# Seven-product experts: another order of products and joins, later sums, a second slot for one weight quarter, an earlier gather

## The reference

```python
def expert_choice_moe(x, w_router, w_gate_up, w_down):
    B, S, _ = x.shape
    cap = CAPACITY_FACTOR * S // N_EXPERTS
    aff = jax.nn.softmax((x @ w_router).astype(jnp.float32), axis=-1)
    gates, idx = lax.top_k(jnp.swapaxes(aff, 1, 2), cap)
    bi = jnp.arange(B)[:, None, None]
    xs = x[bi, idx]
    g, u = jnp.split(jnp.einsum('becd,edf->becf', xs, w_gate_up), 2, axis=-1)
    out = jnp.einsum('becf,efd->becd', jax.nn.silu(g) * u, w_down) * gates[..., None].astype(x.dtype)
    return jnp.zeros_like(x).at[bi, idx].add(out)
```

## Time and profile before

| what | value |
|---|---|
| median of 3 runs | 4094.3 us (4091.58 to 4097.19) |
| profiled execution's own time | 4084.89 us |
| its span | 4083.2 us |
| TensorE busy | 3809.2 us (93%) |
| VectorE busy | 2042.4 us (50%) |
| ScalarE busy | 1127.0 us (28%) |
| GpSimd busy | 470.7 us (12%) |
| mean granted TensorE clock | 0.973 of full |

### The profile page before, as it was taken

How to read it: one execution, slowest core, us unless ns; L and a number is a source line. 1 busy time by engine, 2 the same in 40 slices (tenths; PEclk the granted TensorE clock), 3 DMA queues, 4 the chain that set the end, 5 groups by cost and what they waited for, 6 DMA issues and landing times. The chain is left out here.

```text
span 4083.2 us, 68182 instructions
## 1 busy us (share of the span) xinstructions
PE 3809.2 (93%) x28924; PEld 2006.4 (49%) x28924; DVE 2042.4 (50%) x3704; ACT 1127.0 (28%) x2409; POOL 470.7 (12%) x629
## 2 busy tenths in 40 slices
PE   8999999898989799999979999998999979999998
PEld 5555755757575644545544333333444444333333
DVE  2233334565656511146656566664366557566664
ACT  2343223434343301025531111113343421011113
POOL 3340002111111000000100111110000000111110
PEclk8998999999999999999989999999999989999999
DMA  4001101000100042020049899987211149899997
GB/s 107 27 26 39 33 27 47 9 22 9 27 4 22 4 143 78 11 62 1 1 181 325 298 322 314 315 316 275 74 37 31 52 170 320 282 324 319 326 325 255
DMA packets 271454, 567.51 MB, mean 139 GB/s; under 512 B 53504, under 2 KB 127392, under 8 KB 271152
## 3 DMA queue, kind: packets, MB, share of 16 engines
q1 hardware_dynamic: 255680, 506.01, 36.1%
q0 software_dynamic: 9504, 34.61, 3.2%
q10 hardware_dynamic: 5968, 22.55, 1.4%
HBM read 514.85 MB, written 48.23 MB: 138 GB/s over the span
## 5 line engine op out<-in xcount | busy, mean ns | idle before, releaser
L3618 PE MATMUL bank<-ring,m_hidden_T 128*128 128x512 f32 x1024 | 452.0, 597 | 0.0
L3618 PEld LDWEIGHTS bank<-ring,m_hidden_T 128*128 128x128 f32 x1024 | 192.4, 191 | 248.7 <-issue 248.7
L3618 PE MATMUL bank<-ring,m_picked_T 128*128 128x512 f32 x512 | 233.5, 614 | 4.1 <-ACT m_picked_T L3801 4.1
L1562 PE MATMUL bank<-hnT,first_block 128*128 128x336 f32 (+3 forms) x544 | 182.1, 487 | 8.0 <-PEq L101 7.3
L3631 PE MATMUL bank<-X,m_chosen 128*64 128x512 f32 x768 | 173.2, 604 | 6.3 <-POOL m_chosen L4210 6.3
L3631 PE MATMUL bank<-ring,m_chosen 128*64 128x512 f32 x768 | 174.2, 595 | 0.0
L4012 DVE TENSOR_TENSOR X<-ring 128x1024 f32<-128x1024 f32 x96 | 115.0, 1221 | 100.6 <-DMA ring<-in_moe_w_gate_up 99.7
L3618 PEld LDWEIGHTS bank<-ring,m_picked_T 128*128 128x128 f32 x512 | 99.3, 197 | 126.9 <-issue 121.5
L241 PE MATMUL bank<-xT,first_block 128*128 128x512 f32 x352 | 152.4, 593 | 2.8 <-ACT l_i L3269 1.7
L2825 PE MATMUL bank<-xT,a_weights 128*128 128x512 f32 x320 | 142.3, 595 | 0.8 <-ACT xT L2681 0.8
L1562 PEld LDWEIGHTS bank<-hnT,first_block 128*128 128x128 f32 x544 | 102.2, 193 | 66.0 <-issue 18.8
(11 more groups left out here) (554 smaller groups left out, 7093.7 us busy)
## 6 DMA issues: line engine op xcount, KB each, us to landing
ring<-in_moe_w_gate_up SPq DMA_DIRECT2D x512, 512.0 KB, 7.5
ring<-in_moe_w_down SPq DMA_DIRECT2D x256, 512.0 KB, 5.6
first_block<-in_w_in SPq DMA_DIRECT2D x23, 512.0 KB, 3.9
w_block<-in_w_in SPq DMA_DIRECT2D x19, 512.0 KB, 3.9
x_rows<-X ACTq DMA_DIRECT2D x2, 4096.0 KB, 17.3
ring<-y_rows SPq DMA_DIRECT2D x16, 512.0 KB, 8.7
out_w<-in_w_out ACTq DMA_DIRECT2D x11, 512.0 KB, 12.3
first_block<-in_lru_w_in SPq DMA_DIRECT2D x11, 512.0 KB, 3.9
```

The costliest lines, as they stand in the source:

```text
L1562: m = pe.matmul(banks[j][:, 0:n], wb[i % 3][:, d, :], hnT[:, d, col:col + n], start=d == 0, stop=d == KD - 1)
L3618: m = pe.matmul(banks[j][:, :], lhsT[:, (i % 8) * P:(i % 8 + 1) * P], ring[:, i, j, :], start=i % 8 == 0, stop=i % 8 == KD - 1)
```

## The change

- **Products**: s4b22, s2t2, s1t1, s3t3, 12b21; `turn_tokens(e + 1)`; 22t4; then the first half's transposes, half a product, the second half's. s1t1 goes into the bank of the first product, which first_kept has emptied. Columns 0 to 511 of `hid` are finished first, 512 to 1023 last.
- **Joins** in the order u2, c22's part (u4), 12, u3, 22, 11, 21; the gating of the first half before 22t4's join.
- **Sums**: all of t1, t2 and t3 of e+1 behind the last gating product.
- **Loads**: quarter 0 has a second set of slots (`m_second_ring`, 4 slabs), taken by even experts; it is loaded two experts ahead, slab by slab between down slabs. `landed` grows by 4 semaphores. All eight down slabs of e+1 are loaded as those of e are used.
- **ScalarE**: the first half's sigmoid before the token copies; both copies of the hidden halves after the second sigmoid.
- **GpSimd**: from expert 3 on, the gather of e+2 follows the sums of e+1, ahead of scatter e.

The diff, without its context lines and without the hunks that only pass the expert to `landed_at`, `quarter` and `weight`:

```diff
@@ -3411,7 +3411,7 @@
-        ring = st.sb("ring", [P, SLABS, 2, HALF_FF])
+        ring, second = st.sb("ring", [P, SLABS, 2, HALF_FF]), st.sb("m_second_ring", [P, 4, 2, HALF_FF])
...
@@ -3424,7 +3424,7 @@
-        landed = [st.sem(f"slab_landed{i}") for i in range(SLABS)]
+        landed = [st.sem(f"slab_landed{i}") for i in range(SLABS + 4)]
...
@@ -3449,8 +3449,8 @@
-        PRODUCTS = ("11", "s2t2", "s3t3", "s1t1", "22t4", "12b21", "s4b22")
-        JOINS = ("u2", "u3", "22", "u4", "21", "11", "12")
+        PRODUCTS = ("11", "s4b22", "s2t2", "s1t1", "s3t3", "12b21", "22t4")
+        JOINS = ("u2", "u4", "12", "u3", "22", "11", "21")
...
@@ -3488,9 +3488,15 @@
-        quarter = lambda q, j: ring[:, 4 * q + j, :, :].rearrange("p x c -> p (x c)")
+        place = lambda e, i: SLABS + i if e in SEVEN and e % 2 == 0 and i < 4 else i
+        slot = lambda e, i: (second[:, i, :, :] if place(e, i) >= SLABS else ring[:, i, :, :])
+        quarter = lambda e, q, j: slot(e, 4 * q + j).rearrange("p x c -> p (x c)")
...
+        def landed_at(e, i):
+            at = place(e, i)
+            return landed[at].sem, 16 * sum(place(x, i) == at for x in range(e + 1))
...
         def slab(e, i):
...
@@ -3508,7 +3514,7 @@
         def sync(sp):
             def load(e, i):
-                sp.dma_start(ring[:, i, :, :], slab(e, i)).then_inc(*landed[i].up(16))
+                sp.dma_start(slot(e, i), slab(e, i)).then_inc(*landed[place(e, i)].up(16))
...
@@ -3519,29 +3525,29 @@
+            for i in range(4):
+                load(SEVEN[0] + 1, i)
+            for i in range(20, SLABS):
+                sp.wait_ge(used.sem, used_at(SEVEN[0] - 1, i + 1))
+                load(SEVEN[0], i)
...
-                sp.wait_ge(w_summed.sem, w_summed_at(e, "t3_3"))
-                sp.wait_ge(made.sem, made_at(e, "11"))
-                for i in range(4):
+                sp.wait_ge(w_summed.sem, w_summed_at(e, "t2_3"))
+                sp.wait_ge(made.sem, made_at(e, "s4b22"))
+                for i in range(8, 12):
...
-                for i in range(20, SLABS):
-                    sp.wait_ge(used.sem, used_at(e - 1, i + 1))
-                    load(e, i)
...
+                sp.wait_ge(w_summed.sem, w_summed_at(e, "t4_3"))
...
-                sp.wait_ge(made.sem, made_at(e, "s4b22"))
-                for i in range(8, 12):
-                    load(e + 1, i)
-                for i in range(16, 20):
+                sp.wait_ge(w_summed.sem, w_summed_at(e, "t3_3"))
+                for i in range(16, SLABS):
+                    if e + 2 < NE and i < 20:
+                        load(e + 2, i - 16)
...
-            for i in range(20, SLABS):
-                sp.wait_ge(used.sem, used_at(NE - 2, i + 1))
-                load(NE - 1, i)
...
         def spread_bank(x, t):
...
@@ -3652,43 +3658,40 @@
-                        pe.wait_ge(joined.sem, joined_at(e - 1, "u3"))
-                m = product(first_bank(e), x_quarter(e, 0, 0), weight(0), (lo, hi))
+                        pe.wait_ge(joined.sem, joined_at(e - 1, "22"))
+                m = product(first_bank(e), x_quarter(e, 0, 0), weight(e, 0), (lo, hi))
...
-            def four_products(e):
+            def five_products(e):
...
+                pe.wait_ge(x_summed.sem, x_summed_at(e, "s4"))
+                landed_all(e, 2)
...
+                product(ps[3], summed(3), weight(e, 2)).then_inc(*made.up())
...
-                pe.wait_ge(x_summed.sem, x_summed_at(e, "s2"))
...
+                pe.wait_ge(kept.sem, e - SEVEN[0] + 1)
+                product(first_bank(e), summed(0), weight(e, 1)).then_inc(*made.up())
...
-                product(ps[3], summed(0), weight(1)).then_inc(*made.up())
+                pe.wait_ge(joined.sem, joined_at(e, "u4"))
+                landed_all(e, 3)
+                product(first_bank(e), x_quarter(e, 0, 1), weight(e, 3)).then_inc(*made.up())
...
+            def last_product(e):
...
-            def fifth_product(e):
...
-                pe.wait_ge(kept.sem, e - SEVEN[0] + 1)
-                landed_all(e, 3)
-                product(first_bank(e), x_quarter(e, 0, 1), weight(3)).then_inc(*made.up())
...
-            def last_product(e):
...
-                pe.wait_ge(joined.sem, joined_at(e, "u4"))
-                pe.wait_ge(x_summed.sem, x_summed_at(e, "s4"))
-                landed_all(e, 2)
-                product(ps[3], summed(3), weight(2)).then_inc(*made.up())
...
             def turn_half(e, i):
...
-                    m = pe.transpose(ps[4 + i][:, b * P:(b + 1) * P], hid[:, 512 * (1 - i) + b * P:512 * (1 - i) + (b + 1) * P],
+                    m = pe.transpose(ps[4 + i][:, b * P:(b + 1) * P], hid[:, 512 * i + b * P:512 * i + (b + 1) * P],
...
@@ -3725,11 +3728,10 @@
-                    four_products(e)
+                    five_products(e)
...
-                    fifth_product(e)
+                    last_product(e)
...
-                    last_product(e)
...
@@ -3805,22 +3807,18 @@
             def keep_first(e):
...
-                    ac.wait_ge(acted.sem, 4 * e - 1)
+                    ac.wait_ge(acted.sem, 4 * e - 3)
...
             def sigmoid_half(e, i):
-                if i == 0:
-                    ac.wait_ge(joined.sem, joined_at(e, "21"))
-                    ac.activation(hid[:, 512:1024], c21, ACT.Sigmoid).then_inc(*sig.up())
-                else:
-                    ac.wait_ge(joined.sem, joined_at(e, "11"))
-                    ac.activation(hid[:, 0:512], first_kept[:, :], ACT.Sigmoid).then_inc(*sig.up())
+                ac.wait_ge(joined.sem, joined_at(e, ("11", "21")[i]))
+                ac.activation(hid[:, 512 * i:512 * i + 512], (first_kept[:, :], c21)[i], ACT.Sigmoid).then_inc(*sig.up())
...
             def copy_half(e, i):
...
-                ac.activation(hs[:, :].rearrange("p (s b r t) -> p s b r t", s=2, b=4, r=2)[:, :, :, 1 - i, :],
+                ac.activation(hs[:, :].rearrange("p (s b r t) -> p s b r t", s=2, b=4, r=2)[:, :, :, i, :],
...
             def sigmoid(e, h):
@@ -3851,10 +3849,11 @@
+                    sigmoid_half(e, 0)
...
-                    for i in range(2):
-                        sigmoid_half(e, i)
-                        copy_half(e, i)
+                    sigmoid_half(e, 1)
+                    copy_half(e, 0)
+                    copy_half(e, 1)
...
@@ -4035,40 +4034,34 @@
-                ve.wait_ge(made.sem, made_at(e, "s3t3"))
+                ve.wait_ge(made.sem, made_at(e, "s1t1"))
...
-                ve.tensor_tensor(u3[:, :], third_bank(e)[:, :], u2[:, :], ALU.add).then_inc(*joined.up())
+                ve.tensor_tensor(c22[:, :], first_bank(e)[:, :], u2[:, :], ALU.add).then_inc(*joined.up())
+                ve.wait_ge(joined.sem, joined_at(e, "u4"))
+                ve.tensor_tensor(c12, ps[3][:, :], c22[:, :], ALU.add).then_inc(*joined.up())
...
-                ve.wait_ge(made.sem, made_at(e, "s1t1"))
-                ve.wait_ge(joined.sem, joined_at(e, "u3"))
-                ve.tensor_tensor(c22[:, :], ps[3][:, :], u3[:, :], ALU.add).then_inc(*joined.up())
-                ve.wait_ge(made.sem, made_at(e, "s1t1"))
-                ve.tensor_tensor(u2[:, :], ps[3][:, :], u2[:, :], ALU.add).then_inc(*joined.up())
+                ve.wait_ge(made.sem, made_at(e, "s3t3"))
+                ve.tensor_tensor(u3[:, :], third_bank(e)[:, :], u2[:, :], ALU.add).then_inc(*joined.up())
+                ve.tensor_tensor(c22[:, :], third_bank(e)[:, :], c22[:, :], ALU.add).then_inc(*joined.up())
+                ve.wait_ge(made.sem, made_at(e, "12b21"))
+                ve.tensor_tensor(first_kept[:, :], first_bank(e)[:, :], first_kept[:, :],
+                                 ALU.add).then_inc(*joined.up())
+                ve.wait_ge(joined.sem, joined_at(e, "11"))
+                ve.tensor_tensor(c12, c12, first_kept[:, :], ALU.mult).then_inc(*acted.up())
+                ve.wait_ge(sig.sem, 2 * e + 1)
+                ve.wait_ge(*acted.now())
+                ve.tensor_tensor(hid[:, 0:512], hid[:, 0:512], c12, ALU.mult).then_inc(*acted.up())
...
-                ve.wait_ge(sig.sem, 2 * e + 1)
+                ve.wait_ge(sig.sem, 2 * e + 2)
...
-                    sum_first(e + 1, 0)
-                    sum_first(e + 1, 1)
-                ve.wait_ge(made.sem, made_at(e, "12b21"))
-                ve.tensor_tensor(first_kept[:, :], first_bank(e)[:, :], first_kept[:, :],
-                                 ALU.add).then_inc(*joined.up())
-                if e + 1 in SEVEN:
-                    sum_first(e + 1, 2)
-                    sum_first(e + 1, 3)
-                ve.wait_ge(sig.sem, 2 * e + 2)
-                ve.tensor_tensor(hid[:, 0:512], hid[:, 0:512], first_kept[:, :], ALU.mult).then_inc(*acted.up())
-                ve.wait_ge(made.sem, made_at(e, "s4b22"))
-                ve.tensor_tensor(c12, ps[3][:, :], u2[:, :], ALU.add).then_inc(*joined.up())
-                ve.wait_ge(joined.sem, joined_at(e, "12"))
-                ve.wait_ge(*acted.now())
```

(38 more changed lines are left out.)

## The result

The changed kernel takes 4048.55 us (median of 4 runs, 4044.43 to 4058.52) against 4092.94 for the kernel before in the same comparison: ratio 0.9901, 95% interval 0.9881 to 0.9921, so 32 to 49 us less. Forecast were 4063 (31 less) with a range down to 4056. The direction was right and both waits went, but the size was too small.

What follows compares the result with a forecast made beforehand. The prediction took TensorE, busy 93%, with 31.75 us of idle time over 20 stretches in two waits, as the bound. Steady stretches -29.75 and ends -1.1 made -31: 4094.3 to 4063 us, range 4056 to 4084.

Steps and rivals of the forecast that it cites:

- (1) Gather: Token transposes: gather issued ahead of scatter and transposes after five products remove TensorE's wait, 1.19 us in the expert shown.
- (2) The gate's tail: Second hidden transposes, waiting for the last gating product: wait falls from 0.6 to 0.1 us, bounds 0.0 to 0.6.
- The sum: Whole kernel: steady stretches -29.75 us, ends -1.1, together -31, from 4094.3 to 4063 us.
- up to 3 less: Slow stretches that now find slack: up to 3 us less, given as a bound on the likeliest time.
- stretches of 41.0 us: Sign that the forecast holds: one expert, cut between copies L3810, takes 41.0 us.
- (3), (4) Sums and joins: VectorE's next sums all behind the gating, and joins in the new order: cost nothing.
- (5) Loads: DMA: 38.8 us of work plus 2 unusable fit an expert's 40.98 by a hair; cost 0 to 0.9 us.
- (6) Ends: First and last seven-product experts: expert 3 +0.3 us a layer, expert 14 with the start of 15 -0.85.
- B: GpSimd's token sums starved by VectorE's sums, s4b22 0.75 us late in each expert: 4081 us, chance 0.10.
- C: DMA mildly becomes the bound, every expert pays up to 0.9 us: 4073, at most 4085 us, chance 0.16.
- D: DMA slows to the worst stretch's pace, 44.4 us an expert: 4137 us, slower than before, chance 0.05.
- E: Removed waits open again elsewhere, as at the joins, undoing the gain: 4086 to 4100 us, chance 0.09.

Runs made afterwards that it cites:

- e1: The changed kernel with GpSimd's loop as before, the gather of e+1 behind scatter e-1 again: 4044.86 us.
- e8: The kernel before with the gather ahead of the scatter and t1 sums behind the gating, old order of products, joins and loads: 4048.38 us, ratio 0.991.
- e7: The changed kernel with the token sums of e+1 held until 22t4 is made, instead of s3t3: 4055.26 us.
- e2: The kernel before with only GpSimd's loop changed, the gather ahead of the scatter: 4077.33 us.
- e3: The kernel before with only the four t1 sums moved behind the last gating product: 4072.14 us.
- e6: The changed kernel with two t1 sums (t1_0 and t1_1) put back between the two gating halves: 4068.89 us.
- e9: The changed kernel with the token sums of e+1 held until t1_3 of e+1: 4057.83 us.
- x1: The changed kernel without second slots, with one more 512 KB load an expert that nothing reads, behind quarter 3: 4055.39 us.
- x2: The changed kernel without second slots, with two more 512 KB loads an expert that nothing reads, behind quarter 3: 4051.79 us.

## Why the prediction was right or wrong

**What bounds the kernel** (31.75 us of idle time in two waits): right. It all went.

**(1) Gather.** Its wait went, as said, but the reason given was double. Either five products ahead of the transposes (e1) or the earlier gather (e8) is enough.

**(2) The gate's tail.** The chain was right to 0.1 us. The wait of 0.1 chosen for the meeting of the product with c22 and the last token sum did not appear: they overlap by 0.04 us. That is 2.0 us over 20 stretches. The rows of e7 show what a meeting costs: 1.18 and 1.59 us for token sums of 0.72, and 5.68 for VectorE's 4.62. The Trainium skill, page "SBUF — State Buffer", section "SBUF: two separate sides", has the shared port pair locked for a whole instruction; these rows agree. (A full loss of 0.5 against the 0.1 us of slack would have been a wait of 0.4, not the 0.3 of the prediction.)

**The sum.** The step that failed is "20 x 0.1 - 31.75 = -29.75". It took idle time away and kept TensorE's work at its mean of 41.03 us an expert. Measured is 37.1 us less, with a work of 40.77. The missing 7.4 us are, but for rounding: the tail's 2.0; the excess work of slow stretches, 820.71 - 20 x 40.88 = 3.1; and 20 x (40.88 - 40.77) = 2.2. The last two were on the page as busy time, but belong to the waits. The 3.1 are matmuls at the lower clock behind some of the waits for L4070: in the kernel before after 2.63 and 1.88 us but not after 1.92, in e2 after 2.56, 2.46 and twice 2.03 but not after 2.20 (twice) and another 2.03. And each ordinary wait leaves about 0.05 us that is counted as work: 40.88 with two waits (before), 40.83 with the gather's alone (e3), 40.81 with the gate's alone (e6, e7), 40.77 with none, in the new order and in the old (e8). The 3.1 were even named ("up to 3 less"), as a bound and not in the sum, though the sign to look for, "stretches of 41.0 us", had them in: the sum itself leaves (852.46 - 29.75) / 20 = 41.14 us.

With these 7.4 us the forecast would have been 4056, the very edge of the range. The measured median lies 7.5 us below that: 1.4 by the kernel before (4092.94 instead of 4094.3), 2.6 ahead of the first stretches, 3.8 between the medians and the profiled executions, less 0.2 at the ends. That is scatter, for which the prediction had 3 us where the changed kernel's four runs span 14.

**(3), (4) Sums and joins:** cost nothing, as said. But moving the t1 sums was called free and was the larger part of the gain: with them ahead of the gate a late quarter 1 pushed the gating, which the prediction had seen only as "slow stretches", and even in the others L4070 began 0.2 us later and met a token sum. e3, that move alone, took 19.6 us off the 20 stretches, the gather alone 5.8 (e2).

**(5) Loads.** "It fits, by a hair" was wrong on the margin. Two more slabs fit as well. The DMA share was read as work that adds up, 38.8 us of it with 2 us unusable. It rose from 0.95 to 1.00 for 8% more bytes and left the stretches alone. (The upper bound of 0.9 us does not come out of its term either: 41.4 and 2 less 40.98 are 2.4.)

**(6) Ends.** Expert 3: wait 3.84 us instead of 3.13 (forecast +0.8). Ahead of expert 15 a wait for join 21 of 0.40 (forecast 0.3). Stretches of expert 3: +0.03 and +0.06 us.

**The rivals.** B: not so where it was tried, since GpSimd gets its turn (e7, e9); late sums cost 0.3 us, not 0.75. C and D: false (x1, x2). E: did not come; e2 shows what it would have looked like.

**Left open:** why the first token sum of expert 3 waits for six VectorE operations in a row (7.37 us in both layers of all twelve profiles without the hold), when in e7 and e9 each sum waits for one. It was not tried apart. Nor is it known why the clock falls behind some waits of about 2 us and not behind others.

## What to carry to other kernels

Work that waits for a transfer must not stand on an in-order engine ahead of operations that another engine is waiting for, even if the transfer is nearly always in time; moving it behind them took 19.6 us off by itself, and with an earlier gather all that the new order and the second slots gave. Two waits in one loop are to be priced and removed together, as taking away the first may only bring the loop into the second (5.8 and 19.6 us alone, 37.1 together, over the 20 stretches). A wait's price is the idle time plus what the trace books as work behind it, so a forecast should take the undisturbed work of the state without waits, and where the page has no such state, leave room for it in the range.
